# Token-shift mixing and level masks on VectorE, in one step of a hybrid decoder

## What is computed

```
proj = einsum('btd,de->bte', h, w_in);  rp = proj[..., FOX_IN:]
shifted = concatenate([prev[:, None, :], p[:, :-1]], axis=1)      # p = rp
xm = p + (shifted - p) * mu                                       # token shift
...
def step(S, inp):                                                 # for each token
    sa = einsum('bhvk,bhk->bhv', S, -kk_t)
    S = S * w_t + sa[..., None] * (kk_t * a_t) + v_t[..., None] * k_t
    return S, einsum('bhvk,bhk->bhv', S, r_t)
```

## Time and profile before

| | us |
|---|---|
| median of 3 runs (lowest, highest) | 2087.73 (2085.66, 2091.4) |
| the profiled execution | 2089.39 |
| its span, first to last instruction | 2087.5 |
| outside the span | 1.9 |
| busy: TensorE products | 1784.7 |
| busy: VectorE, ScalarE, GpSimd | 413.1, 249.6, 192.6 |
| mean granted TensorE clock, as a share of 2.4 GHz | 0.898 |

### The profile page before, as it was taken

The page is one execution under the profiler, slowest core; times in us unless marked ns, Lnnn a source line. Parts: engine busy times, 40 slices in busy tenths (PEclk is TensorE's granted clock), DMA queues, the critical chain, the costliest instruction groups (busy, mean ns, idle before and its releaser), DMA issues.

```text
span 2087.5 us, 25877 instructions
## 1 busy us (share of the span) xinstructions
PE 1784.7 (85%) x10676; PEld 1305.8 (63%) x10677; DVE 413.1 (20%) x726; ACT 249.6 (12%) x491; POOL 192.6 (9%) x207
## 2 busy tenths in 40 slices
PE   6997696557799999789769999789999799997784
PEld 3765354455577777564349999339995389953331
DVE  2013524964211111562000000000001000010002
ACT  2121243011200000231000001010001000010101
POOL 4003502662000000030000000000000000000001
PEclk8998586565899999989979999999999999999897
DMA  9751042000735555704985555999779997889995
GB/s 340 270 199 62 24 122 53 3 1 26 271 131 202 202 182 197 256 12 150 390 311 212 211 200 195 354 391 357 275 268 338 390 389 256 289 313 389 392 391 214
DMA packets 235292, 481.61 MB, mean 231 GB/s; under 512 B 16575, under 2 KB 90691, under 8 KB 234803
## 3 DMA queue, kind: packets, MB, share of 16 engines
q1 hardware_dynamic: 229755, 471.91, 62.5%
q0 software_dynamic: 3904, 5.44, 0.8%
q10 hardware_dynamic: 1568, 3.34, 0.4%
HBM read 473.12 MB, written 7.90 MB: 230 GB/s over the span
## 4 chain that ended last, share of the span: by engine, by line
PE 69%; DMA 16%; DVE 5%; POOL 4%; issue 3%; SPq 2%; ACT 2%; POOLq 0%; ACTq 0%; DVEq 0%
PE bank L1004 67%; DMA ring<-in_moe_w_up 14%; POOL ring L2197 2%; DMA ring<-in_ada_w 1%; POOL other L2206 1%; ACT ring L1486 1%; SPq L2319 1%; SPq L2284 0%; DVE ring L1870 0%; DVE ring L1861 0%; DVE wide L1778 0%; DVE wide L1762 0%; SPq L836 0%; PE bank L1137 0%; DVE wide L2087 0%
## 5 line engine op out<-in xcount | busy, mean ns | idle before, releaser
L1004 PE MATMUL bank<-wide,ring 128*128 128x144 f32 (+4 forms) x4240 | 696.9, 332 | 27.9 <-issue 15.6
L1004 PEld LDWEIGHTS bank<-wide,ring 128*128 128x128 f32 (+2 forms) x4240 | 618.4, 191 | 106.1 <-issue 40.2
L1004 PE MATMUL bank<-ring,wide 128*64 128x384 f32 (+2 forms) x1600 | 295.0, 525 | 89.7 <-DMA ring<-in_moe_w_up 75.4
L1004 PE MATMUL bank<-other,ring 128*128 128x144 f32 (+3 forms) x2016 | 290.8, 317 | 48.9 <-POOL ring L2197 28.6
L1004 PEld LDWEIGHTS bank<-other,ring 128*128 128x128 f32 (+1 forms) x2016 | 266.4, 191 | 73.9 <-POOL ring L2197 30.2
L1004 PEld LDWEIGHTS bank<-ring,wide 128*64 128x64 f32 (+1 forms) x1600 | 122.8, 158 | 250.5 <-issue 231.9
L1004 PE MATMUL bank<-ring,other 128*64 128x512 f32 x560 | 128.0, 596 | 8.4 <-ACT other L729 8.4
L795 DVE TENSOR_TENSOR other<-other,bank 128x288 f32<-128x288 f32 (+3 forms) x48 | 21.4, 446 | 500.5 <-PE bank L1004 500.5
L777 DVE TENSOR_TENSOR other<-other,bank 64x512 f32<-64x512 f32 (+1 forms) x40 | 24.5, 612 | 458.5 <-ACT other L726 458.5
L2263 POOL TENSOR_TENSOR small<-const 128x1 f32<-128x1 f32 x1 | 0.2, 193 | 1136.3 <-DMA expert_rows<-other 1136.3
L1004 PE MATMUL bank<-ring 128*64 128x64 f32 (+6 forms) x468 | 77.7, 398 | 13.4 <-ACT ring L1486 8.8
(11 more groups left out here) (331 smaller groups left out, 998.1 us busy)
## 6 DMA issues: line engine op xcount, KB each, us to landing
ring<-in_moe_w_gate SPq DMA_DIRECT2D x32, 2048.0 KB, 13.0
ring<-in_moe_w_up SPq DMA_DIRECT2D x32, 2048.0 KB, 16.7
ring<-in_moe_w_down SPq DMA_DIRECT2D x32, 2048.0 KB, 16.8
ring<-in_ada_w SPq DMA_DIRECT2D x24, 2048.0 KB, 14.0
ring<-in_moe_w_gate SPq DMA_DIRECT2D x32, 1536.0 KB, 12.5
ring<-in_moe_w_up SPq DMA_DIRECT2D x32, 1536.0 KB, 16.3
ring<-in_moe_w_down SPq DMA_DIRECT2D x32, 1536.0 KB, 16.4
ring<-in_w_in SPq DMA_DIRECT2D x5, 2048.0 KB, 12.5
```

Of the source, the lines that this page charges most:

```text
L1004: return pe.matmul(out, lhsT, rhs, start=start, stop=stop, skip_group_check=True)
```

## The change

Both edits move work from GpSimd (and ScalarE) to VectorE.

The mixing is done in four groups, each behind the part of the input projection that makes its pieces (`mix_pieces`). VectorE does all of it: copies of the last rows, differences, multiply-adds by mu, one per piece. `lastP` and `lastS` have SBUF of their own.

The mask of a level is no longer laid on the triangle before the first product but on the product, as it leaves PSUM. The masks of levels 1 to 5 are transposed for that. GpSimd masks only at level 0 (`nm`). ScalarE's copies to `xb` are gone: VectorE copies at level 0 and multiplies by the mask at the others. GpSimd's value-key products stand behind its level-0 work, two per pair.

```
@@ VectorE, input projection
+            def mix_pieces(done, i0, n):
+                dve.wait_ge(s("win_act"), done // 2)
+                x, d = rp[:, i0:i0 + n, :], diff[:, 0:n, :]
+                final = i0 + n == NPC
+                do(dve.tensor_copy(lastP[:, i0:i0 + n], x[:, :, NP - 1]))
+                do(dve.tensor_copy(lastS[:, i0:i0 + n, :], x[:, :, NP + NT - 1:N:NT]), once.give("last_ready") if final else chain)
+                do(TT(d[:, :, 1:N], x[:, :, 0:N - 1], x[:, :, 1:N], ALU.subtract))
+                do(TS(d[:, :, 0], x[:, :, 0], -1.0, None, ALU.mult))
+                prev = vT[:, 2, NB * i0:NB * (i0 + n)].rearrange("p (c b) -> p c b", c=n)
+                do(TT(d[:, :, NP:N:NT], prev, x[:, :, NP:N:NT], ALU.subtract))
+                for c in range(n):
+                    do(STT(x[:, c, :], d[:, c, :], vT[:, 1, VB_MU + i0 + c:VB_MU + i0 + c + 1], x[:, c, :], ALU.mult, ALU.add),
+                       once.give("rp_mixed") if final and c == n - 1 else chain)
...
+                if cs[0][0] == "r":
+                    mix_pieces(n, cs[0][1], len(cs))
                 if i:
                     mod_tile(0, 3 + i)
...
-            do(dve.tensor_copy(lastP, rp[:, :, NP - 1]))
-            do(dve.tensor_copy(lastS, rp[:, :, NP + NT - 1:N:NT]), once.give("last_ready"))
@@ GpSimd, mixing
-            pool.wait_ge(s("win_dve"), (len(WCHUNKS) + 1) // 2)
-            pool.wait_ge(s("win_act"), len(WCHUNKS) // 2)
-            pool.wait_ge(*once("last_ready"))
-            me.step(pool.tensor_tensor(diff[:, :, 1:NP], rp[:, :, 0:NP - 1], rp[:, :, 1:NP], ALU.subtract), s("pool_chain"))
...
-            me.step(pool.tensor_tensor(diff, diff, spread(vT[:, 1, VB_MU:VB_MU + NPC], 2, N), ALU.mult), s("pool_chain"))
-            me.step(pool.tensor_tensor(rp, rp, diff, ALU.add), once.give("rp_mixed"))
@@ TensorE, invert
-                        pe.wait_ge(s("nm_ready"), kth(n, lv) + 1)
                         if lv:
                             pe.wait_ge(s("t_ready"), t_count(n, lv - 1))
+                        else:
+                            pe.wait_ge(s("nm_ready"), n + 1)
...
-                            last = mm(b[o, L * c:L * (c + 1)], nm[o, i, c, :], rhs, True, True)
+                            lhs = nm[o, i, c, :] if lv == 0 else gt[o, i, h, 0:L]
+                            last = mm(b[o, L * c:L * (c + 1)], lhs, rhs, True, True)
@@ ScalarE, inversion
-                for lv in range(LEVELS):
-                    for n in (2 * pair, 2 * pair + 1):
-                        act.wait_ge(s("x_mm"), kth(n, lv) + 1)
-                        copy(xb[:, n % 2].rearrange("p h k -> p (h k)"), banks[f"x_{LEVELS * n + lv}"][:, 0:HC * L], s("xb_ready"))
@@ VectorE, inversion
                 for lv in range(LEVELS):
                     for n in (2 * pair, 2 * pair + 1):
+                        dve.wait_ge(s("x_mm"), kth(n, lv) + 1)
+                        x = banks[f"x_{LEVELS * n + lv}"][:, 0:HC * L].rearrange("p (c t) -> p c t", c=HC)
+                        if lv == 0:
+                            do(dve.tensor_copy(xb[:, n % 2], x), s("xb_ready"))
+                        else:
+                            do(TT(xb[:, n % 2], x, spread(K("levels")[:, L * lv:L * (lv + 1)], 1, HC), ALU.mult), s("xb_ready"))
+                    for n in (2 * pair, 2 * pair + 1):
                         i = n % 2
@@ GpSimd, inversion
-            after_level = {(0, 1): 0, (0, 4): 1, (1, 1): 2, (1, 3): 3}
...
-                for lv in range(1, LEVELS):
-                    for n in both:
-                        pool.wait_ge(s("x_mm"), kth(n, lv - 1) + 1)
-                        if lv == 1:
-                            pool.wait_ge(s("t_ready"), t_count(n, 0))
-                        level(n, lv)
-                    if (pair, lv) in after_level:
-                        value_key(after_level[pair, lv])
+                for t in range(2):
+                    value_key(2 * pair + t)
```

More of the change, by code:

```diff
@@ L92, in constants @@
     put("eyes", (s == t) * 1.0)
-    put("levels", np.concatenate([((s // (2 * m) == t // (2 * m)) & (s // m % 2 == 0) & (t // m % 2 == 1)) * 1.0
+    put("levels", np.concatenate([((s // (2 * m) == t // (2 * m)) & ((s if m == 1 else t) // m % 2 == 0)
+                                   & ((t if m == 1 else s) // m % 2 == 1)) * 1.0
                                   for m in (1 << i for i in range(LEVELS))], 1))
@@ L178 @@
 ONCE = {
-    "vector": ("vec_copied vec2_copied k_ready q_ready lf_abs lf_one logf_ready negF_ready last_ready "
+    "vector": ("vec_copied vec2_copied k_ready q_ready last_ready rp_mixed lf_abs lf_one logf_ready negF_ready "
               "kk_scaled rk_ready cum_ready psm_shifted psm_ready delta_ops packed final_state gn_centred "
@@ L184 @@
     "tensor": ("c_turned vec_turned vec2_turned lf_turned last_turned so_mm fst_mm syt_mm route_mm rank_mm"),
-    "gpsimd": ("vrow_zero silucT_zero last_zero rp_mixed zv_ready tables_zero pad_zero"),
+    "gpsimd": ("vrow_zero silucT_zero last_zero zv_ready tables_zero pad_zero"),
 }
@@ L379, in build_program @@
         lfrow = R.cut(3, H)
-        lastS = R.cut(NPC, NB)
-        lastP = R.cut(NPC)
+        lastS = sb("lastS", [P, NPC, NB])
+        lastP = sb("lastP", [P, NPC])
         lastrow = R.cut(2, P)
@@ L1113, in _ @@
             b = banks.open(pe, "last", (s("last_copied"), 2))
-            pe.transpose(b[0:NPC * 8, 0:P], lastS.rearrange("p a b -> p (a b)"), ident)
-            pe.transpose(b[0:NPC, P:2 * P], lastP, ident).then_inc(once.give("last_turned"), 1)
+            pe.transpose(b[0:NPC * 8, 0:P], lastS[:, :, :].rearrange("p a b -> p (a b)"), ident)
+            pe.transpose(b[0:NPC, P:2 * P], lastP[:, :], ident).then_inc(once.give("last_turned"), 1)
             def scores(c, qb):
@@ L1642, in _ @@
                             copy(of(dst[o, n % 2], a_), of(vt[o], a_), s("vt_ready") if a_ and dst is su else chain)
-                for lv in range(LEVELS):
-                    for n in (2 * pair, 2 * pair + 1):
-                        act.wait_ge(s("x_mm"), kth(n, lv) + 1)
-                        copy(xb[:, n % 2].rearrange("p h k -> p (h k)"), banks[f"x_{LEVELS * n + lv}"][:, 0:HC * L], s("xb_ready"))
[L1647 to L1651, removed]
+                if pair == 0:
+                    for a_ in range(2):
+                        for c in range(HC):
+                            copy(lu[own(a_), :, 2 * c + a_, :], ar[own(a_), c, :, 0, :], s("lu_own"))
                 for n in (2 * pair, 2 * pair + 1):
@@ L2190, in _, with level @@
                         once.give("zv_ready") if a_ else s("pool_chain"))
-            def level(n, lv):
+            def level(n):
                 for a_ in range(2):
                     o = own(a_)
-                    mask = spread(K("levels")[o, L * lv:L * (lv + 1)], 1, HC)
+                    mask = spread(K("levels")[o, 0:L], 1, HC)
                     me.step(pool.tensor_tensor(nm[o, n % 2], of(gt[o, n % 2], a_)[:, :, 0:L], mask, ALU.mult),
@@ L2214, in _ @@
                     pool.wait_ge(s("gt_ready"), 2 * n + 2)
-                    level(n, 0)
+                    level(n)
                 for n in both:
```

8 lines of the change are left out of this document (removed).

## The result

| | before | after |
|---|---|---|
| median of 11 runs (lowest, highest), us | 2087.58 (2085.58, 2091.4) | 2094.21 (2092.11, 2095.79) |
| the profiled execution, its span | 2089.39, 2087.5 | 2094.2, 2092.3 |
| busy: TensorE products | 1784.7 | 1781.6 |
| busy: VectorE, ScalarE, GpSimd | 413.1, 249.6, 192.6 | 417.2, 239.9, 108.1 |

The ratio is 1.0032, with a 95% interval of 1.0023 to 1.0041: slower by 6.6 us, 0.3%. GpSimd's busy time fell by 44%, and the kernel got no faster.

The account below looks back on a forecast made before the run. TensorE and expert-weight loads hold most of the chain; the edits touch only 100 to 511 us. Part one -15.0 and part two +17.2 gave +2 us: 2091.5 against the profiled execution, about 2090 against the median, range 2078 to 2098.

Parts of the forecast that it names:

- part two: Inversion, masks on VectorE: mask, products and additions no longer run beneath sample operations; +17.2 us.
- part one: Mixing on VectorE: hidden in the input projection, and GpSimd's holds at the attention's start go; -15.0 us.
- Mixing hidden: Input projection: VectorE's mixing fits its gaps, the last group ending at 184.8 before TensorE is done at 185.14; cost zero.
- Holds gone: -15.0: Attention's start: two softmax operations no longer wait for GpSimd's mixing, saving 6.73 and 8.31 us.
- Masks in front of the products: Inversion levels: 4.4 us exposed mask, products and additions plus 6.96 of sample operations; first pair +10.3 us.
- Second pair: +6.9: Inversion, second pair: the same levels, with additions held by GpSimd's third value-key product; +3.4 if that holds nobody.
- the bounds of 1.8 and 23.2: Part two's limits: +1.8 us with fast products and no hold, +23.2 with all at 1.2 GHz and one more hold.
- the fourth hold: Second pair, upper bound only: the fourth value-key product goes in front of a sample operation, +3.6 us.
- Rival 1: Inversion: products run fast and holds don't come, part two +1.8, net -13, 2075 us; chance 0.14.
- rival 3: Attention: its steady half also regains the 2.4 GHz clock, perhaps 10 us less, net -8, 2080 us; chance 0.06.
- rival 2: Second pair: both value-key products go ahead of VectorE operations, all products at 1.2 GHz; +8, 2096 us; chance 0.15.
- Rival 4: Input projection: mixing not hidden, a last group 2 us longer moves everything by 1.9; total +4; no separate chance given.

Follow-up runs that it names:

- the part alone: Two runs against the kernel before: only the mixing on VectorE, 2071.19 us, ratio 0.9919; only the masks on VectorE, 2110.45 us, ratio 1.0107.
- the additions that nobody reads: The changed kernel plus three two-input GpSimd additions of unused result at the attention's start: 2106.1 us, ratio 1.0079 to the kernel before.
- two-and-one kernel: The changed kernel with two of a level's three sample operations between masks and additions, one behind the additions: 2083.6 us, ratio 0.9977 to the kernel before.
- the copies: The changed kernel plus three one-input GpSimd copies of unused result at the attention's start: 2098.06 us, ratio 1.0042 to the kernel before.

## Why the prediction came out as it did

The forecast was about 2090 us with a range of 2078 to 2098, and no change as the likeliest. Measured: 2094.2, slower by 0.32%, just over the 0.3% that the forecast took as its limit; it had given that side a chance of 0.22. Both mechanisms were those forecast, but the sum of part two was too small by 5.5 us. That the total missed by only 4 is in part luck: part one gave 1.6 us more than its sum by the time of the part alone, and no term of the forecast stands for that.

- **Mixing hidden.** Right. The last group ends at 185.12, where the forecast had 184.8. This execution was 0.4 us late there; from the end of ScalarE's last copy it is 3.7 us where the forecast had 3.8. The last modulation tile still waits for TensorE 0.22 us. A full group took 4.5 us, not 4.8 (a multiply-add 0.54, not 0.46; the long difference 1.35, not 1.84).
- **Holds gone: -15.0.** Right: -14.6 in the profile, -16.6 in the time of the part alone, 14.8 of it in that kernel's profile by the attention's end. That it is the engine and not the data was shown by the additions that nobody reads.
- **Masks in front of the products: a level of 4.4 + 6.96 us.** The mechanism was right, the size short. I had the last product of a level run fast. In the first pair all four ran at 1.2 GHz, with TensorE idle 6.3 to 6.8 us before each level (11.5 before level 1), and a level's exposed part was 4.7. Over four levels that is the 1.3 us between the 11.6 measured and the 10.3 forecast; level 5 took the 3.0 forecast. The long idle stretch can't be the whole reason: in the two-and-one kernel TensorE paused 1.7 to 2.3 us at a time (371.70 to 393.45), and the granted clock was 0.50 too.
- **The term that was missing.** Level 5 is followed by one more product and ScalarE's copy of it. Before, they stood at 402.33, well ahead of the state's chain (407.01), beneath sample operations. Now they come at 400.14, between the last products and the state's chain at 401.75, and are bare: +1.4 in the first pair, +1.8 in the second, where 0.4 more is the clock of the chain's first product (0.68 us at 489.16 before, 1.12 at 493.19 after). The forecast put this term at nothing by leaving it out. Its size is read from the traces; no run moved that product. I had counted what stands ahead of VectorE's operations, and not what TensorE had behind its own. TensorE before, then after:

```profile
402.33 1.12 PE L1004 MATMUL bank<-ring 128*64 128x64 f32 x16
407.01 1.12 PE L1004 MATMUL bank<-ring,wide 64*64 64x64 f32 x16 [3.56 <-issue]
```

```profile
400.14 1.12 PE L1005 MATMUL bank<-ring 128*64 128x64 f32 x16
401.75 1.12 PE L1005 MATMUL bank<-ring,wide 64*64 64x64 f32 x16 [0.48 <-ACT ring L1489]
```

- **Second pair: +6.9.** It was +7.9, with the hold as forecast (3.72 us at 433.52). The fourth value-key product did not fall beneath masks and additions, as forecast, but beside a sample operation; it cost nothing all the same, since VectorE had started first (451.77 against 451.88). The levels are 11.7 us, the low clock again.
- **Sum of part two: +17.2.** It was +22.7 by the profile (11.6 + 1.4 + 7.9 + 1.8) and +22.7 by the part alone, within the bounds of 1.8 and 23.2 and at their far end. The bounds left out the missing term as well; they held because the fourth hold, 3.6 of the 23.2, did not come.
- **Rival 1** (products fast) and **rival 3** (attention at full clock) did not come: the granted clock was 0.50 in the attention, in the same stretch of all eleven profiles, with TensorE busy 32 of 38 us, and 0.62 to 0.64 in the inversion. Of **rival 2** one condition came, the products at 1.2 GHz, and that accounts for some 2.4 us by its own sum. The other didn't. The time came near its 2096 by the missing term, not by its mechanism. **Rival 4** did not come.

What I had seen but not weighed: the earlier trace rows showed VectorE full in the first pair, and the change put a chain through it one link at a time, with its fillers outside the chain. The fillers' place was worth 27 us there, more than either part (with the masks on GpSimd it was 7.5: 2071.2 to 2063.7).

## What to carry to other kernels

When a step moves onto the engine that also runs the filler work, move the filler too: here it belonged between a step and its answer, not behind the answer. Ask of every such move what the other engine had running beneath the old wait, down to the last product behind the loop. And an engine that is off the critical path can still hold another by its operands alone, so look for operations that end just after another engine's.

## What the runs showed of the hardware

- A VectorE operation with two SBUF operands that started while GpSimd was in a long operation waited for its end and then took about its own time. Those of 0.42 and 0.69 us ended 0.3 to 0.55 us after GpSimd's, whether GpSimd's had two inputs (2.17, 4.97, 6.84 us) or one (2.66, 1.86); those of 2.29 us ended 2.14 us after it (4.96 us at 362.56, behind GpSimd's of 361.76 to 365.38). The reduction (one input, 0.69 us at 200.52 and 199.35) and the operations with an operand in PSUM ran free beside both. GpSimd waits in the same way: its product of 3.62 us took 5.66 when it started 0.11 us behind VectorE's operation. Its masks in the kernel before show the same: 48 of them took 0.72 us in the median, up to 2.69, and 1.37 in the mean, some 31 us more than at the median, which the profile counts as busy time. The Trainium skill, "SBUF — State Buffer", section SBUF: two separate sides, has the pair of ports that the two engines share as an exclusive lock: whoever starts first keeps it for its whole instruction, and a VectorE operation needs it when it has two SBUF inputs. By that rule it doesn't matter how many inputs GpSimd's operation has, and the copies agree; my expectation for them did not. That the first to start wins agrees with 451.77 and 451.88.
- TensorE's granted clock differs between executions at the same place: 4.21 and 2.20 us for six products in two profiles of the kernel before, 10.91 and 8.04 for 36 products in two kernels with the same program up to there. The stage from the attention's end to the cleared tile took 82.2 to 82.7 us at a mean of 0.83 and 85.0 to 86.5 at 0.78 to 0.80. A difference of that size in one profile of each kernel is not evidence.
- In every level of the changed kernel, with TensorE idle 4.4 to 11.5 us before it, the products between masks and additions began at 1.2 GHz, and nearly all stayed there (1.06 us for 16). With pauses of only 1.7 to 2.3 us, in the two-and-one kernel, they did so too.
